# Latent attention's opening: low part of the latent in three pieces, gate chunks and sample scores regrouped

## The reference, cut to what matters

```python
ckr = rmsnorm(x, kv_norm) @ w_dkv
c = rmsnorm(ckr[..., :KV_LORA], kv_lat_norm)            # the latent, 256 wide
kr = rope(ckr[..., KV_LORA:][:, :, None, :], pos)       # one rotary key, 64 wide
q = (rmsnorm(p[..., :Q_LORA], b_q_norm) @ b_w_uq).reshape(..., 8, 128 + 64)
k_nope, v = split((c @ w_ukv).reshape(..., 8, 256))
logits = (q_nope . k_nope + rope(q_rope) . kr) * MLA_SCALE
o = softmax(logits) @ v
x = x + (o * silu(p[..., Q_LORA:])) @ b_w_out
```

## Time and profile before

| | |
|---|---|
| three runs | 1333.64, 1335.52 (median), 1339.07 us |
| the profiled execution | 1329.36 us |
| its span, first to last instruction | 1327.6 us |
| TensorE's mean granted clock in it | 0.995 |
| matmuls | busy 1276.5 us, 8573 instructions |
| VectorE, ScalarE, GpSimd busy | 705.3, 435.9, 517.6 us |

### The profile page before, as it was taken

The page is one execution under the profiler, slowest core; times in us unless marked ns, Lnnn a source line. Parts: engine busy times, 40 slices in busy tenths (PEclk is TensorE's granted clock), DMA queues, the critical chain, the costliest instruction groups (busy, mean ns, idle before and its releaser), DMA issues. The chain is left out here.

```text
span 1327.6 us, 21463 instructions
## 1 busy us (share of the span) xinstructions
PE 1276.5 (96%) x8573; PEld 1235.9 (93%) x8573; DVE 705.3 (53%) x1368; ACT 435.9 (33%) x843; POOL 517.6 (39%) x548
## 2 busy tenths in 40 slices
PE   6999999999999999999999999999999999999996
PEld 6999999999999999989999999889999999998996
DVE  7456462446344443565334488455665666666145
ACT  6324232223222222343114233243443344335111
POOL 2344343525162425153666656502122122127522
PEclk9999999999999999999999999999999999999998
DMA  6231212222131211033413138902211211124312
GB/s 215 95 105 53 77 56 88 67 71 76 52 97 45 89 57 61 25 153 127 167 67 114 52 107 271 277 9 71 59 41 50 75 50 46 50 61 177 147 51 83
DMA packets 54515, 120.65 MB, mean 91 GB/s; under 512 B 12416, under 2 KB 29440, under 8 KB 54160
## 3 DMA queue, kind: packets, MB, share of 16 engines
q1 hardware_dynamic: 51696, 110.24, 25.1%
q0 software_dynamic: 2432, 8.78, 2.4%
q10 hardware_dynamic: 288, 0.26, 0.1%
HBM read 80.57 MB, written 35.89 MB: 88 GB/s over the span
## 5 line engine op out<-in xcount | busy, mean ns | idle before, releaser
L83 PE MATMUL psum<-act,fox_slot_hi 128*128 128x358 f32 (+1 forms) x552 | 182.9, 331 | 10.2 <-DVE act L991 10.2
L84 PE MATMUL psum<-act,fox_slot_hi 128*128 128x358 f32 (+1 forms) x552 | 180.2, 326 | 0.0
L85 PE MATMUL psum<-act,fox_slot_lo 128*128 128x358 f32 (+1 forms) x552 | 180.0, 326 | 0.0
L1317 POOL TENSOR_SCALAR fox_rows<-fox_f_keys,fox_f_query 128x144 f32<-128x144 f32 (+3 forms) x64 | 50.5, 790 | 191.8 <-PE psum L692 188.1
L83 PEld LDWEIGHTS psum<-act,fox_slot_hi 128*128 128x128 f32 x552 | 104.1, 189 | 10.2 <-DVE act L991 10.2
L84 PEld LDWEIGHTS psum<-act,fox_slot_hi 128*128 128x128 f32 x552 | 104.2, 189 | 0.0
L85 PEld LDWEIGHTS psum<-act,fox_slot_lo 128*128 128x128 f32 x552 | 104.1, 189 | 0.0
L881 ACT ACTIVATE fox_pT_hi<-psum 128x512 fp32r<-128x512 f32 (+3 forms) x112 | 52.3, 504 | 103.3 <-PE psum L692 103.2
L859 ACT ACTIVATE fox_rows<-fox_rows,fox_neg_max 128x144 f32<-128x144 f32 (+3 forms) x64 | 50.6, 790 | 97.1 <-DVE fox_neg_max L1072 96.2
L83 PE MATMUL psum<-fox_slot_hi,act 128*128 128x256 f32 (+1 forms) x288 | 81.1, 282 | 0.0
L85 PE MATMUL psum<-fox_slot_hi,act 128*128 128x256 f32 (+1 forms) x288 | 81.0, 281 | 0.0
(11 more groups left out here) (392 smaller groups left out, 3937.6 us busy)
## 6 DMA issues: line engine op xcount, KB each, us to landing
fox_x<-in_xT SPq DMA_DIRECT2D x8, 536.0 KB, 9.1
out<-fox_key SPq DMA_DIRECT2D x8, 536.0 KB, 2.7
mix_resid<-in_xT SPq DMA_DIRECT2D x8, 536.0 KB, 3.9
resid_b<-mix_resid SPq DMA_DIRECT2D x8, 536.0 KB, 2.9
q_nope<-mla_nope SPq DMA_DIRECT2D x8, 536.0 KB, 5.6
mla_query<-q_nope SPq DMA_DIRECT2D x8, 536.0 KB, 3.9
mla_end_y<-resid_b SPq DMA_DIRECT2D x8, 536.0 KB, 6.2
fox_f_keys<-f_cum SPq DMA_DIRECT2D x8, 520.0 KB, 4.3
```

Source lines behind the costliest of these rows:

```text
L83: pe.matmul(out, lh, rh, start=start and k == 0, stop=False)
L84: pe.matmul(out, lh, rl, start=False, stop=False)
L85: last = pe.matmul(out, ll, rh, start=False, stop=stop and k == n - 1)
L1317: chain(pool.tensor_scalar(row[:, KEY_META:KEY_META + live], f_keys[h % 2][:, 0:live], 1.0, f_query[:, i + 1, h:h + 1], ALU.mult, ALU.add))
```

## The change

The low part of the latent is made in three column pieces (376, 348 and 348 columns of each half), each with a signal of its own; key chunk c waits for piece c, and ScalarE's key roundings for all three. The three gate chunks follow each other on PE, ahead of `turn_own` and `absorb`. On ScalarE the first gate chunk's tanh stands ahead of `round_last_rope`; on VectorE the first `gate_take` stands ahead of `last_rope`, and `gate_mul` between `last_rope` and `last_rope_rest`. The tiles of the cached keys become 32 columns longer, ScalarE copies the own keys into these columns (two new copies, signal `own_beside`), and `sample_scores` makes two groups of 272 columns for each half of the queries.

```diff
+    c_parts = [(KEY0, KEY_FIRST + W3), (KEY_FIRST + W3, KEY_FIRST + 2 * W3), (KEY_FIRST + 2 * W3, KEYS)]
...
-        cache_rT, small_q, small_rope = at(100544, "cache_rT", [ROPE, PAST]), at(102592, "small_q", [P, HEADS, N_SAMPLE]), at(103616, "small_rope", [ROPE, HEADS, N_SAMPLE])
+        cache_rT, small_q, small_rope = at(100544, "cache_rT", [ROPE, PAST + N_SAMPLE]), at(102720, "small_q", [P, HEADS, N_SAMPLE]), at(103744, "small_rope", [ROPE, HEADS, N_SAMPLE])
...
-        cache_cT, cache_nat = at(44160, "cache_cT", [P, KC, PAST]), at(48256, "cache_nat", [P, NC, KV_LORA])
+        cache_cT, cache_nat = at(44160, "cache_cT", [P, KC, PAST + N_SAMPLE]), at(48512, "cache_nat", [P, NC, KV_LORA])
...
             pool.wait_ge(rope_ready, 3)
-            pool.tensor_tensor(c_lo[:, :, KEY0:KEY0 + T], latent[:, :, :], c_hi[:, :, KEY0:KEY0 + T].bitcast(F32), ALU.subtract).then_inc(c_split, 1)
+            for a, b in c_parts:
+                pool.tensor_tensor(c_lo[:, :, a:b], latent[:, :, a - KEY0:b - KEY0], c_hi[:, :, a:b].bitcast(F32), ALU.subtract).then_inc(c_split, 1)
...
-            sp.dma_start(cache_rT[:, :], dram.cache_rT).then_inc(cache_loaded, 16)
+            sp.dma_start(cache_rT[:, 0:PAST], dram.cache_rT).then_inc(cache_loaded, 16)
...
-            sp.dma_start(cache_cT[:, :, :], dram.cache_cT).then_inc(cache_loaded, 16)
+            sp.dma_start(cache_cT[:, :, 0:PAST], dram.cache_cT).then_inc(cache_loaded, 16)
...
-                    if h == 0:
-                        pe.wait_ge(c_split, 1)
+                if h == 0:
+                    pe.wait_ge(c_split, c + 1)
...
                 pe.wait_ge(own_taken, 1)
+                pe.wait_ge(own_beside, 2)
                 pe.wait_ge(cache_loaded, 80)
                 for g in range(2):
                     q = slice(P * g, P * g + P)
-                    for n, (b, c, w, cached, kc) in enumerate(((2 * g, 0, S_HALF, True, 0), (2 * g + 1, 0, PAST - S_HALF, True, S_HALF),
-                                                               (2 * g + 1, PAST - S_HALF, N_SAMPLE, False, 0))):
-                        out = bank[b][:, c:c + w]
+                    for n in range(2):
+                        out, keys = bank[2 * g + n][:, 0:S_HALF], slice(S_HALF * n, S_HALF * n + S_HALF)
                         for k in range(KC):
-                            keys = cache_cT[:, k, kc:kc + w] if cached else c_own[:, k, :]
-                            pe.matmul(out, absorbed[:, k, q], keys, start=k == 0, stop=False)
-                        keys = cache_rT[:, kc:kc + w] if cached else rope_own[:, :]
-                        last = pe.matmul(out, small_rope[:, :, :].rearrange("p h n -> p (h n)")[:, q], keys, start=False, stop=True)
+                            pe.matmul(out, absorbed[:, k, q], cache_cT[:, k, keys], start=k == 0, stop=False)
+                        last = pe.matmul(out, small_rope[:, :, :].rearrange("p h n -> p (h n)")[:, q], cache_rT[:, keys], start=False, stop=True)
...
-            gate_chunk(0, 0)
-            gate_chunk(0, 1)
+            for c in range(3):
+                gate_chunk(0, c)
             turn_own()
             absorb()
-            gate_chunk(0, 2)
             sample_scores()
...
             act.wait_ge(c_stored, 32)
+            act.wait_ge(c_split, len(c_parts))
             for c in range(3):
                 key_chunk(0, c)
+            gate_chunk(0, 0)
             round_last_rope()
-            gate_chunk(0, 0)
             split_query(0)
             act.wait_ge(own_turned, 1)
+            act.wait_ge(taken, USES * PAIRS)
+            act.activation(cache_cT[:, :, PAST:PAST + N_SAMPLE], c_own[:, :, :], ACT.Copy).then_inc(own_beside, 1)
+            act.activation(cache_rT[:, PAST:PAST + N_SAMPLE], rope_own[:, :], ACT.Copy).then_inc(own_beside, 1)
...
             latents_dve(dve, key_chunk)
+            gate_take(0, 0)
             last_rope()
+            gate_mul(0, 0)
             last_rope_rest()
-            gate_take(0, 0)
-            gate_mul(0, 0)
             split_query(0)
```

More of the change, by code:

```diff
@@ L1588, in latent_attention @@
         nope_stored, few_stored, rope_stored = [sem("nope_stored0"), sem("nope_stored1")], sem("few_stored"), sem("rope_stored")
-        kw_first, g_first, own_turned, own_taken = sem("kw_first"), sem("g_first"), sem("own_turned"), sem("own_taken")
+        kw_first, g_first, own_turned, own_taken, own_beside = sem("kw_first"), sem("g_first"), sem("own_turned"), sem("own_taken"), sem("own_beside")
         proj_full, proj_free = [sem("proj_full0"), sem("proj_full1")], [sem("proj_free0"), sem("proj_free1")]
```

## The result

The changed kernel takes 1337.41 us (median; 1332.15 to 1340.66), the kernel before, run beside it, 1334.01 us (1331.03 to 1339.07). The ratio is 1.0026, 95% interval 1.0015 to 1.0037: by that ratio **slower by 3.5 us** (2.0 to 4.9). That is inside the 0.5% that I called no change and inside the range, but the sign is the other one: I had forecast 0.6 us faster.

What follows compares the result with a forecast made beforehand. TensorE, busy 1276.5 of 1327.6 us, was taken as the bound. PE's own work came 1.5 us earlier, the rotary transfer 0.6; the later decides, so 1335.52 less 0.6 gives 1334.9 us, range 1331.5 to 1339.0.

Steps and rivals of the forecast that it cites:

- The pieces: Latent's low part on GpSimd, three subtractions, 5.2 us in sum; first gate chunk at 829.1 instead of 829.82, gain 0.7 us.
- The gate chunks together: On PE, three chunks at 3.93 us; the 0.36 us w_ukT wait goes, 0.69 us charged ahead of the sample scores.
- The small rotary transfer: Last small transfer the sample scores wait for; lands at 846.1, so they start at 846.2 against 847.55.
- the moved take: VectorE's take of the first gate chunk, freeing its bank for the third; at 833.2 to 833.7, 7 us ahead of need.
- Own keys beside the cached: Sample scores on PE in two groups per half: 6.68 instead of 8.44 us, 1.76 us saved; ScalarE's copies cost 0.
- The low clock: PE's 1.2 GHz level behind the absorption: its 1.6 us cost moves from third gate chunk to score stage, unchanged.
- rival C: Low clock holds the whole score stage, 13.4 us; first prompt scores 3.6 us later, 1339.1 us; chance 0.07.
- The last rotation and the rotary tiles: Stores leave GpSimd 1.0 us earlier, rotary tile lands 0.6 us earlier at 857.3; first prompt scores at 857.45.
- which earlier stores can use: Transfer engines stood empty 0.66 us in the last 2 us before the stores landed; earlier stores could use this.
- rival B: Stores land only with the whole transfer batch, loads stay at 848.76, no gain: 1335.4 us; chance 0.25.

Runs made afterwards that it cites:

- the extra float32 work of 128 and of 64 rows: Changed kernel plus twelve extra plain float32 356-column matmuls, of 128 rows or of 64 rows, ahead of the sample scores; two kernels, each executed once, no ratio.
- half the chunk: Changed kernel with half of the third gate chunk (12 of 24 matmuls) put behind the absorption; 1332.22 us, ratio 0.9999 to the kernel before.
- the woven one: Changed kernel with the absorption's 32 narrow matmuls placed between the third gate chunk's 24 dense ones; 1332.97 us, ratio 1.001 to the kernel before.
- the fastest kernel: Woven absorption, plus rotary load and value split before GpSimd's wait for stores, third prompt scores before sample values, sample-output wait later; 1330.3 us, ratio 0.9981 to before.

## Why the prediction was wrong

*The pieces*: right. 5.12 us for three (5.2 worked out), the first key chunk at once, 0.70 us ahead of the third, the gate 3.92 us after the query products (4.15 worked out).

*The gate chunks together*: right, 0.71 us ahead of the scores for the 0.69 charged, no wait for w_ukT. The small rotary transfer, which I let decide the scores' start at 846.2, did not: they started 0.9 us earlier, when ScalarE was done (with the extra float32 work of 128 and of 64 rows, in the same order, it did decide, by 1.64 and 0.86 us). One reading was wrong: the moved take is not "7 us ahead of need" but 3.3, since the third chunk starts at 829.1 + 7.86. It was in time.

*Own keys beside the cached*: right. ScalarE's two copies, 0.26 and 0.21 us, lie under the absorption, and at 1.00 the stage takes 6.96 to 6.98 us for the 6.68 worked out.

***The low clock*: this step failed.** "I move the 1.6 us there: it neither goes nor grows." It moved there and grew, from 3.4 us low to 13.65. The stage took 12.0 us where I had 6.7 + 1.6 = 8.3. I had treated the low level as a spell of fixed length, whoever runs in it. The rows showed two falls of about 3.5 us, but both ended under dense 128-row work; what the scores do when they meet the low level themselves, no row showed. The runs showed it: with 64 rows in a third of their matmuls they stay at 0.50, and with those rows padded by zeros the stage takes 5.64 us at 1.00. My argument against rival C, that these matmuls ran at 1.00 soon after a fall, showed only that they keep a level they are given.

*The last rotation and the rotary tile*: half right. The stores left 0.8 us earlier as worked out (841.34 less 3.4), but the loads left 0.7 us later than before instead of 0.6 earlier (852.87 less 3.4, against 848.76): "which earlier stores can use" was wrong, and rival B nearer. It cost nothing, because PE came later still. Where PE was in time the wait was there: 1.95 and 2.15 us with half the chunk and with the woven one, and none with the load freed and the clock at 1.00: in the fastest kernel the first prompt scores start 30.2 us after the query products without a wait, in the woven one 32.0.

*Rival C*, at 0.07, is what happened. It gave 3.6 us; the ratio says 3.5. That agreement is in part luck: the stage took 12.0 us, not 13.4, since its first 1.4 us ran at 1.00, and the sample values, on which it was silent, lost 1.5 us to a longer second fall. It deserved more: the rows had two falls behind narrow matmuls, and the edit took away what stood behind one of them. The measured time lies in the range only because the range allows for scatter up to 1339.0; that it "also holds most of C" was wrong, since C itself stood at 1339.1.

Still open: why the second fall, under the sample values, lasts 3.4, 6.8 or 10.2 us in different kernels (no run was made for it); why the first, behind the absorption, lasts 3.4, 6.8 or 10.2 us with the gate chunk behind it, and does not come at all in some kernels; and what the padded rows are worth together with the moved rotary load and value split; that was not tried.

## What to carry to other kernels

A dense stretch between narrow matmuls and matmuls of few rows can be doing a second job, bringing the clock back; before moving it, ask which work will then meet the low level, and whether that work has been seen to raise it. Half the chunk left in place, narrow matmuls woven into dense ones with dense ones at the end, or few-row operands padded with zero rows each gave the scores the full clock. The weave alone does not keep the clock from falling: it fell for 6.83 us in three of the six woven profiles. When a hole is closed, look up the next transfer: w_ukT, the sample queries, the rotary tile and GpSimd's value weights each became the bound in turn.

## What was unexpected of the hardware

A busy PE can stay at 1.2 GHz: 14.49 of 14.74 us busy with 64-row matmuls, at 0.50, in a low stretch of 30.72 us, where 128-row matmuls of the same form and columns came back to 1.00 after 6.83 us. Rows of zeros did as well as filled ones (5.64 and 5.69 us for the score stage).

Padding also made the matmuls quicker at the same clock. Two groups of the scores at 1.00, the fastest kernel's with its 64-row pair first, the padded kernel's behind:

```profile
849.47 1.18 PE L2455 MATMUL psum<-mla_cache_cT,mla_absorbed 128*128 128x272 f32 x4
850.58 0.72 PE L2456 MATMUL psum<-mla_cache_rT,mla_small_rope 64*128 64x272 f32 x2
851.23 1.18 PE L2455 MATMUL psum<-mla_cache_cT,mla_absorbed 128*128 128x272 f32 x4
```
```profile
849.13 1.08 PE L2441 MATMUL psum<-mla_cache_cT,mla_absorbed 128*128 128x272 f32 x4
850.05 0.62 PE L2442 MATMUL psum<-mla_cache_rT,mla_small_rope 128*128 128x272 f32 x2
850.51 1.08 PE L2441 MATMUL psum<-mla_cache_cT,mla_absorbed 128*128 128x272 f32 x4
```

From start to start a group takes 1.76 and 1.38 us. The 0.38 us more lie half in the four 128-row instructions and half in the pair behind them. The Trainium skill (TensorE: Matmul & The Clock Gate, section "Why this matters for your kernels") says that a single matmul with 32 contraction rows takes the same time as one with 128. The extra work agrees for 64 rows in a row: 24 instructions take 14.50 us at 0.50, 0.60 us each, and those of 128 rows, 5.78 us at 0.50 and 4.34 at 1.00, come to 0.60 us each at 0.50 too. So the price seems to be that of changing between 128 and 64 rows, not of the 64-row matmul itself.
